# Dense sub-blocks: transposing the raw residual and scaling gate and up by a broadcast row

## The chip, the cores and the metric

One core of one Trainium2 chip runs the whole program. The metric is the device time of one execution in microseconds (us). Engines: TensorE (PE; its weight loads are PEld), VectorE (DVE), ScalarE (ACT), GpSimd (POOL) and SyncE (SP), which issues the weight loads by DMA.

## The reference

The input is 256 tokens of 1024 numbers in float32. Two blocks of two layers follow each other. In the first block each layer is a dense SwiGLU (d_ff 2816), a mixer, and a second SwiGLU, each with an RMS norm before and after it:

```python
def rms_norm(x, g):
    xf = x.astype(jnp.float32)
    return xf * lax.rsqrt(jnp.mean(xf * xf, axis=-1, keepdims=True) + NORM_EPS) * g.astype(jnp.float32)
...
        hdn = swiglu(rms_norm(x, norm_pre[l, 2]), ffn2_w_gate[l], ffn2_w_up[l], ffn2_w_down[l])
        x = x + 0.5 * rms_norm(hdn, norm_post[l, 2])
```

SwiGLU is (silu(h Wg) * (h Wu)) Wd. The norm divides every token by one number, so with r = 1/rms of a token, h Wg = r * ((x*g) Wg), and the same for Wu. The second block (modulated mixers, a dense SwiGLU of 3584, a mixture of eight experts) needs modulation vectors, c_act @ mod_w + mod_b, which are worked out beside the first block.

## The kernel before

The program is a list of ten sub-blocks, `SUBS`: 0, 2, 3 and 5 are the dense SwiGLUs of the first block ("ffn", 22 units of 128 hidden columns each), 1 ("ab") and 4 ("c") its mixers, 6 to 9 the second block. Every engine's instruction stream is written out by hand in program order, with semaphores between them; nothing is rescheduled, so an instruction that waits holds all that stands behind it on its engine.

Every number goes to TensorE as a high and a low part (`XH`, `XL` for the transposed residual, `wh_*`, `wl_*` for weights, `HH`, `HL` for the hidden activations), and each product is three matmuls (`mm3`, L1721 to L1723): high by high, high by low, low by high. A weight block arrives by DMA in `raw_gu` or `raw_d` (two buffers each); ScalarE makes the high part (`hi_gu` L395, `hi_d` L402) and VectorE the low part (`lo_gu` L857, `lo_d` L862).

The start of a dense sub-block b, `pre(b)`:

1. ScalarE squares each of the two token tiles of the residual `X` (`squares`, L413) and takes the root (`root`, L420), then loads the SiLU table (`load_table`, L430).
2. VectorE takes the reciprocal (L948) and writes it on a diagonal, `RS_DIAG` (L954).
3. TensorE multiplies X by that diagonal (L1779): a transpose with the scale in it, 8 pieces of 128 by 128 for each token tile, each of them two passes in the trace. They go to PSUM (`turned`): tile 0 to two banks, tile 1 to four.
4. ScalarE copies each piece to `XH` times the norm's gain (L453), VectorE makes `XL` (L963). They do this in the groups of `TURNS`: four and four pieces of tile 0, then four times two of tile 1. The first gate/up product may begin once the first group of tile 1 is done (`xt_l`).

The loop `ffn`: for unit n TensorE forms gate and up into bank n % 2 of `PB` (`gate_up`, 48 matmuls of 256 columns), ScalarE takes SiLU of the gate (L523), VectorE multiplies it by up (L1070), splits the result (L1071, L1072), and TensorE adds the unit's down product into `PA` (`down`, 12 matmuls of 512 columns). TensorE's order is gate_up(n+1), down(n), so a unit's down product comes a whole gate_up later; only the last down product has no gate_up ahead of it.

GpSimd works out the modulation sums (`modulation`) beside sub-blocks 0, 2, 3 and 4 to 5; it begins them when the transposed residual of that sub-block is complete, in sub-block 0 also after ScalarE's `c_act` (L457). TensorE turns them into columns (`mod_columns`, L1808), behind the last down product of sub-blocks 0, 2 and 3 and ahead of it in sub-block 5. `post(b)` multiplies by the gain, takes the second norm and adds to the residual (L1021, L1025).

Plain transposes, of data that need no diagonal, are at L1781; sub-blocks 6 to 9 use them.

## Time and profile before

| what | value |
|---|---|
| runs (3) | 2750.99, 2751.63, 2753.77 us; median 2751.63 |
| profiled execution, span from first to last instruction | 2747.2 us |
| TensorE busy | 2600.3 us, 95% |
| VectorE, ScalarE, GpSimd busy | 79%, 54%, 34% |
| granted TensorE clock, mean | 0.971 of full |
| loop of sub-block 0, 32 to 206 us | TensorE busy 173.97 of 174.00 us |

The time around the span cannot be read from the trace; the median of the runs stands 4.4 us above the span. TensorE is at work nearly all the time and idle mainly between sub-blocks. A busy share says nothing of whether its clock was full: the column PEclk gives that, as a share of 2.4 GHz.

### The profile page before, as it was taken

What the parts mean: (1) busy time and instruction counts of PE and PEld (TensorE: products, weight loads), DVE (VectorE), ACT (ScalarE), POOL (GpSimd) and SP (SyncE); (2) the same over time, 40 slices, a digit from 0 to 9 for tenths busy, and PEclk for the clock granted to TensorE, in tenths of its full rate; (3) what the DMA queues carried; (4) which work ended last, traced back from release to release, by engine and by line L of the source; (5) the groups of instructions that cost most, each with busy time, mean ns of one, the idle gap of its engine ahead of it and who ended that gap; (6) DMA issues with size and microseconds to landing.
All of it is one profiled execution on the core that took longest, in us unless ns stands there. A gap on an engine that the chain in (4) does not pass through costs nothing. (4 is left out here: it accounts for less than half of the span.)

```text
span 2747.2 us, 47482 instructions
## 1 busy us (share of the span) xinstructions
PE 2600.3 (95%) x17802; PEld 2379.0 (87%) x17802; DVE 2165.5 (79%) x2488; ACT 1483.6 (54%) x1930; POOL 947.8 (34%) x586
## 2 busy tenths in 40 slices
PE   8999899999998998888998978999999999999997
PEld 7999699999897998658998747999999999999986
DVE  5667666766787676987855997898989898989888
ACT  4337543443434334424334515777777777777765
POOL 6990089688789992126900130000000000000000
PEclk9999999999999998999999988999999999999999
DMA  8664267566566653324553415999999999999985
GB/s 309 252 237 148 103 241 256 202 250 254 191 241 229 220 183 134 115 105 164 183 184 138 164 63 192 343 350 333 352 335 349 338 347 343 347 345 346 340 320 216
DMA packets 129209, 670.58 MB, mean 244 GB/s; under 512 B 14672, under 2 KB 14992, under 8 KB 80064
## 3 DMA queue, kind: packets, MB, share of 16 engines
q1 hardware_dynamic: 111024, 604.72, 59.9%
q0 software_dynamic: 18064, 64.21, 6.9%
q8 instruction: 81, 1.33, 0.2%
q14 instruction: 40, 0.33, 0.0%
HBM read 667.82 MB, written 1.05 MB: 243 GB/s over the span
## 5 line engine op out<-in xcount | busy, mean ns | idle before, releaser
L1721 PE MATMUL work<-xT_hi,wh_gu 128*128 128x256 f32 x2088 | 593.9, 284 | 21.6 <-DVE xT_lo L985 12.0
L1722 PE MATMUL work<-xT_lo,wh_gu 128*128 128x256 f32 x2088 | 592.3, 284 | 0.0
L1723 PE MATMUL work<-xT_hi,wl_gu 128*128 128x256 f32 x2088 | 591.7, 283 | 0.0
L1721 PE MATMUL work<-wh_gu,mixT_hi 128*128 128x256 f32 x1792 | 507.5, 283 | 2.8 <-DVE wl_gu L1439 1.5
L1722 PE MATMUL work<-wl_gu,mixT_hi 128*128 128x256 f32 x1792 | 505.8, 282 | 0.0
L1723 PE MATMUL work<-wh_gu,mixT_lo 128*128 128x256 f32 x1792 | 505.5, 282 | 0.0
L857 DVE TENSOR_TENSOR wl_gu<-raw_gu,wh_gu 128x2048 fp32r<-128x2048 f32 x158 | 392.3, 2483 | 72.0 <-ACT wh_gu L395 71.5
L1721 PEld LDWEIGHTS work<-xT_hi,wh_gu 128*128 128x128 f32 x2088 | 401.3, 192 | 30.1 <-issue 21.3
L1722 PEld LDWEIGHTS work<-xT_lo,wh_gu 128*128 128x128 f32 x2088 | 401.7, 192 | 4.8
L1723 PEld LDWEIGHTS work<-xT_hi,wl_gu 128*128 128x128 f32 x2088 | 401.5, 192 | 0.0
L862 DVE TENSOR_TENSOR wl_d<-raw_d,wh_d 128x1024 fp32r<-128x1024 f32 x157 | 250.2, 1594 | 189.6 <-ACT wh_d L402 189.5
L1721 PE MATMUL acc<-wh_d,h_hi 128*128 128x512 f32 x912 | 380.4, 417 | 2.8 <-DVE wl_d L1444 2.7
L1723 PE MATMUL acc<-wh_d,h_lo 128*128 128x512 f32 x912 | 361.2, 396 | 0.0
L1722 PE MATMUL acc<-wl_d,h_hi 128*128 128x512 f32 x912 | 361.1, 396 | 0.0
L1721 PEld LDWEIGHTS work<-wh_gu,mixT_hi 128*128 128x128 f32 x1792 | 340.9, 190 | 12.5 <-DVE wl_gu L1439 1.7
L1722 PEld LDWEIGHTS work<-wl_gu,mixT_hi 128*128 128x128 f32 x1792 | 341.6, 191 | 8.8
L1723 PEld LDWEIGHTS work<-wh_gu,mixT_lo 128*128 128x128 f32 x1792 | 341.5, 191 | 0.0
L402 ACT ACTIVATE wh_d<-raw_d 128x1024 fp32r<-128x1024 f32 x157 | 166.2, 1059 | 276.1 <-PE acc L1723 276.1
L395 ACT ACTIVATE wh_gu<-raw_gu 128x2048 fp32r<-128x2048 f32 x158 | 300.7, 1903 | 25.4 <-PE acc L1723 25.0
L1652 POOL TENSOR_SCALAR scratch<-scratch,small 128x1024 f32<-128x1024 f32 x84 | 312.9, 3724 | 4.2
L1439 DVE TENSOR_TENSOR wl_gu<-raw_gu,wh_gu 128x2048 fp32r<-128x2048 f32 x113 | 259.1, 2293 | 38.0 <-ACT wh_gu L726 37.9
L1439 DVE TENSOR_TENSOR wl_gu<-scratch,wh_gu 128x2048 fp32r<-128x2048 f32 x112 | 256.6, 2291 | 25.5 <-ACT wh_gu L726 25.0
(436 smaller groups left out, 4785.6 us busy)
## 6 DMA issues: line engine op xcount, KB each, us to landing
raw_gu<-in_w_gu SPq DMA_DIRECT2D x271, 1024.0 KB, 5.2
raw_d<-in_w_d SPq DMA_DIRECT2D x269, 512.0 KB, 5.4
scratch<-in_w_gu SPq DMA_DIRECT2D x112, 1024.0 KB, 7.2
scratch<-in_w_d SPq DMA_DIRECT2D x112, 512.0 KB, 7.8
scratch<-in_w_mod POOLq DMA_DIRECT2D x96, 512.0 KB, 3.7
scratch<-in_s_b POOLq DMA_DIRECT2D x16, 256.0 KB, 2.9
rows<-in_norm_post POOLq DMA_DIRECT2D x6, 512.0 KB, 4.4
rows<-in_ln_g POOLq DMA_DIRECT2D x4, 512.0 KB, 5.5
```

The source lines that it names most:

```text
L395: act.activation(wh_gu[k][:, :, :, :].rearrange("p a k n -> p (a k n)"), raw_gu[k][:, :], ACT.Copy).then_inc(gu_hi, 1)
L402: act.activation(wh_d[k][:, :], raw_d[k][:, :], ACT.Copy).then_inc(d_hi, 1)
L857: TT(wl, raw_gu[k][:, :], wh.bitcast(F32), ALU.subtract).then_inc(gu_lo, 1)
L862: TT(wl_d[k][:, :], raw_d[k][:, :], wh_d[k][:, :].bitcast(F32), ALU.subtract).then_inc(d_lo, 1)
L1439: TT(wl, RAW_GU[k] if k > 1 else RAW_GU[k][:, :], wh.bitcast(F32), ALU.subtract).then_inc(gu_lo, 1)
L1652: link(pool.tensor_scalar(MW[n % 3], MW[n % 3], c, None, ALU.mult))
L1721: pe.matmul(out_, w[0], m[0], start=start, stop=False)
L1722: pe.matmul(out_, w[0], m[1], start=False, stop=False)
L1723: return pe.matmul(out_, w[1], m[0], start=False, stop=stop)
```

## The change

In the dense sub-blocks of the first block (`RAW_FFN` = 0, 2, 3, 5):

- TensorE transposes the raw X (plain transposes) as soon as x_in or x_first and x_done allow. There is no `RS_DIAG` for them.
- ScalarE squares tile 0, makes `XH`, then splits the weight block of the sub-block's second unit, squares tile 1, takes both roots and loads the SiLU table.
- VectorE, in its first step, takes both reciprocals behind `lo_gu` of the second unit (`token_scales`). TensorE forms from them a 128 by 256 block with every row the scales of the 256 tokens (`scale_row`, two float32 products into bank 3), between gate_up of the first and of the second unit, and VectorE copies it to `RS_ROW`.
- In every unit VectorE multiplies gate by `RS_ROW` (to `SG`) and up by `RS_ROW` (to `HF`), ScalarE takes SiLU of `SG` in place, and VectorE multiplies the two.
- `mod_columns(1)` moves ahead of the last down product of sub-block 2.

The diff, cut:

```diff
 ScalarE, pre(b)
+                    own_squares(0)
+                    if b not in RAW_FFN:
+                        root(eps_rms, 0)
+                        own_squares(1)
+                        root(eps_rms, 1)
                     if b == 0:
                         act.wait_ge(cols_in, 16)
                         hi_gu(0)
...
+                    if b in RAW_FFN:
+                        hi_gu(START[b] + 1)
+                        own_squares(1)
+                        for t in range(NT):
+                            root(eps_rms, t)
+                        load_table(ACT.Silu)
                     if b == 0:
                         act.activation(c_act, C("c", 0, KD), ACT.Silu).then_inc(c_act_done, 1)
                         hi_d(0)
 ScalarE, ffn
+                        if b in RAW_FFN:
+                            ge(act, gate_scaled, SCALED[b] + n - n0 + 1, at)
+                            act.activation(SG[n % 2], SG[n % 2], ACT.Silu).then_inc(silu_done, 1)
 VectorE
+            def token_scales():
+
+                for t in range(NT):
+                    roots[0] += 1
+                    dve.wait_ge(root_done, roots[0])
+                    dve.reciprocal(rs[:, t:t + 1], rs[:, t:t + 1]).then_inc(rs_ready, 1)
+                scale_rows[0] += 1
+                dve.wait_ge(rs_ps, scale_rows[0])
+                link(dve.tensor_copy(RS_ROW, PB[:, 3, 0:S]))
...
                     lo_gu(n + 1, j)
+                    if first:
+                        token_scales()
+                    if raw:
+                        ge(dve, gu_used, n + 1, j)
+                        TT(SG[k], PB[:, k, 0:S], RS_ROW, ALU.mult).then_inc(gate_scaled, 1)
+                        link(TT(HF[k], PB[:, k, S:2 * S], RS_ROW, ALU.mult))
+                        dve.wait_ge(silu_done, j + (f0 + r + 1))
+                        link(TT(HF[k], SG[k], HF[k], ALU.mult))
 TensorE
+            def scale_row():
+
+                scale_rows[0] += 1
+                pe.wait_ge(rs_ready, NT * scale_rows[0])
+                for t in range(NT):
+                    last = pe.matmul(PB[:, 3, t * P:(t + 1) * P], rs[:, t:t + 1].broadcast_to([P, P]), ident,
+                                     start=True, stop=True)
+                last.then_inc(rs_ps, 1)
...
                 gate_up(n0, dyn)
+                if n0 < START[SECOND]:
+                    scale_row()
                 gate_up(n0 + 1, dyn)
...
-                if n0 == MOD_START[3]:
-                    mod_columns(3)
+                if n0 in (MOD_START[1], MOD_START[3]):
+                    mod_columns(MOD_START.index(n0))
                 down(n0 + nf - 1, dyn, f0 + nf - 1, fdyn, False, True)
-                if n0 in MOD_START[0:3]:
+                if n0 in (MOD_START[0], MOD_START[2]):
```

Where instructions stand, before and after. ScalarE at the program's start, before: squares and roots come first, and behind the pieces of the transposed residual stand `c_act`, the down block of unit 0 and the weight block of unit 1.

```order
L413 ACT_TABLE_LOAD [waits x_in0]
L413 ACTIVATE scratch,small<-residual 128x1024 [waits small_ready]
L420 ACT_TABLE_LOAD
L420 ACTIVATE small<-small 128x1 [waits sq_done]
L413 ACTIVATE scratch,small<-residual 128x1024 [waits sq_done,x_in1]
...
L453 ACTIVATE xT_hi<-acc,cols 128x128
L457 ACTIVATE small<-cols 128x8
L402 ACTIVATE wh_d<-raw_d 128x1024 [waits d_landed0]
L395 ACTIVATE wh_gu<-raw_gu 128x2048 [waits gu_landed1]
L523 ACTIVATE scratch<-work 128x256 [waits gu_used]
```

The same place after:

```order
L466 ACTIVATE xT_hi<-acc,cols 128x128
L404 ACTIVATE wh_gu<-raw_gu 128x2048 [waits gu_landed1]
L422 ACTIVATE scratch,small<-residual 128x1024 [waits sq_done,x_in1]
L429 ACT_TABLE_LOAD
L429 ACTIVATE small<-small 128x1 [waits sq_done] x2
L439 ACT_TABLE_LOAD
L439 ACTIVATE small<-small 128x1 [waits small_ready]
L476 ACTIVATE small<-cols 128x8
L411 ACTIVATE wh_d<-raw_d 128x1024 [waits d_landed0]
L545 ACTIVATE scratch<-scratch 128x256 [waits gate_scaled]
```

The weight block of unit 1 moved ahead of `c_act` and the down block; tile 1's squares, both roots and the table loads moved behind it. VectorE at the program's start, before:

```order
L948 RECIPROCAL small<-small 128x1 [waits root_done,cols_in]
L954 TENSOR_SCALAR scratch<-const,small 128x128 [waits dve_step]
L948 RECIPROCAL small<-small 128x1 [waits root_done]
L954 TENSOR_SCALAR scratch<-const,small 128x128 [waits dve_step]
L857 TENSOR_TENSOR wl_gu<-raw_gu,wh_gu 128x2048 [waits gu_hi]
```

And after, behind the pieces of the transposed residual (`lo_d(0)` stays in `pre`, ahead of the loop's first `lo_gu`):

```order
L989 SCALAR_TENSOR_TENSOR xT_lo<-acc,cols,xT_hi 128x128
L887 TENSOR_TENSOR wl_d<-raw_d,wh_d 128x1024 [waits d_hi]
L882 TENSOR_TENSOR wl_gu<-raw_gu,wh_gu 128x2048 [waits gu_hi]
L1090 RECIPROCAL small<-small 128x1 [waits root_done] x2
L1093 COPY scratch<-work 128x256 [waits rs_ps]
```

Both reciprocals stand behind the two weight pieces now; before they were VectorE's first work. TensorE from the last down product of sub-block 2 to the first product of sub-block 3, before:

```order
L1722 MATMUL acc<-wl_d,h_hi 128x512
L1723 MATMUL acc<-wh_d,h_lo 128x512
L1808 MATMUL work<-small,scratch 128x1 [waits mod_sums]
L1808 MATMUL work<-small,scratch 128x1 x23
L1779 MATMUL work<-scratch,residual 128x128 [waits xn_done]
L1779 MATMUL work<-scratch,residual 128x128 x7
L1779 MATMUL work<-scratch,residual 128x128 [waits mod_copied,xn_done]
```

After:

```order
L1855 MATMUL work<-small,scratch 128x1 [waits mod_sums]
L1855 MATMUL work<-small,scratch 128x1 x23
L1765 MATMUL acc<-wh_d,h_hi 128x512 [waits h_ready,d_lo]
L1766 MATMUL acc<-wl_d,h_hi 128x512
...
L1767 MATMUL acc<-wh_d,h_lo 128x512
L1828 MATMUL work<-const,residual 128x128 [waits x_first]
L1828 MATMUL work<-const,residual 128x128 x7
L1828 MATMUL work<-const,residual 128x128 [waits mod_copied,x_done]
```

The 24 column products moved from behind the last down product to ahead of it, and the transposes wait for the residual itself.

## Rows read from the trace of the kernel before

**Rows 1.** Page, busy us (share of the span) x instructions of each engine.

```profile
PE 2600.3 (95%) x17802; PEld 2379.0 (87%) x17802; DVE 2165.5 (79%) x2488; ACT 1483.6 (54%) x1930; POOL 947.8 (34%) x586
```

**Rows 2.** Loop of sub-block 0: busy by stretch, then VectorE groups (busy, mean ns).

```profile
32.00:206.00 174.00, 173.97 (x1215) 162.28 (x1214) 115.72 (x101) 67.44 (x63) 159.67 (x64) 1.00 0.69 250
...
L1072 DVE TENSOR_TENSOR h_lo<-scratch,h_hi 128x256 fp32r<-128x256 f32 x20 | 9.4, 471 | 0.7
L1070 DVE TENSOR_TENSOR scratch<-scratch,work 128x256 f32<-128x256 f32 x20 | 8.4, 419 | 13.4 <-ACT scratch L523 13.4
```

**Rows 3.** Timeline of the start: start us, duration us, engine, line, [idle before].

```profile
9.89 1.28 ACT L430 ACT_TABLE_LOAD   x1
...
17.19 1.17 ACT L402 ACTIVATE wh_d<-raw_d 128x1024 fp32r<-128x1024 f32 x1
...
18.72 1.92 ACT L395 ACTIVATE wh_gu<-raw_gu 128x2048 fp32r<-128x2048 f32 x1 [0.36 <-DMA raw_gu<-in_w_gu]
...
19.57 1.22 DVE L862 TENSOR_TENSOR wl_d<-raw_d,wh_d 128x1024 fp32r<-128x1024 f32 x1
...
20.70 2.29 DVE L857 TENSOR_TENSOR wl_gu<-raw_gu,wh_gu 128x2048 fp32r<-128x2048 f32 x1
...
24.28 0.39 ACT L523 ACTIVATE scratch<-work 128x256 f32<-128x256 f32 x1 [3.64 <-PE work L1723]
```

**Rows 4.** Timeline of the seam into sub-block 2, ScalarE and TensorE.

```profile
339.39 1.06 ACT L413 ACTIVATE scratch<-residual 128x1024 f32<-128x1024 f32 x1
...
340.57 0.29 ACT L420 ACTIVATE small<-small 128x1 f32<-128x1 f32 x1
...
343.76 1.13 ACT L453 ACTIVATE xT_hi<-work,cols 128x128 fp32r<-128x128 f32 x4
...
348.30 0.36 PE L1721 MATMUL work<-xT_hi,wh_gu 128*128 128x256 f32 x1
```

**Rows 5.** Stretches: length, busy PE, PEld, DVE, ACT, POOL; PEclk, DMA share, GB/s.

```profile
341.50:346.80 5.30, 5.29 (x25) 5.29 (x25) 1.87 (x8) 4.79 (x15) 0.18 (x1) 0.50 0.29 99
...
1058.50:1063.80 5.30, 5.30 (x13) 3.80 (x13) 1.99 (x6) 0.98 (x2) 0.00 (x0) 0.50 0.00 0
...
1074.20:1078.10 3.90, 3.88 (x18) 3.90 (x19) 2.62 (x6) 3.64 (x5) 0.55 (x1) 0.50 0.22 58
...
1249.10:1252.20 3.10, 3.07 (x14) 3.10 (x15) 1.82 (x6) 2.70 (x4) 0.00 (x0) 0.50 0.00 0
...
1504.30:1508.20 3.90, 3.83 (x18) 3.87 (x19) 2.62 (x6) 3.68 (x5) 0.00 (x0) 0.50 0.00 0
```

**Rows 6.** Timeline of the seam into sub-block 5, VectorE and TensorE.

```profile
856.18 3.18 DVE L1025 SCALAR_TENSOR_TENSOR residual<-scratch,small,residual 128x1024 f32<-128x1024 f32 x1
...
867.53 0.36 PE L1721 MATMUL work<-xT_hi,wh_gu 128*128 128x256 f32 x1 [0.22 <-DVE xT_lo L963]
...
869.88 3.57 DVE L857 TENSOR_TENSOR wl_gu<-raw_gu,wh_gu 128x2048 fp32r<-128x2048 f32 x1 [0.95 <-ACT wh_gu L395]
```

**Rows 7.** Timeline of TensorE at the seams into sub-blocks 3 and 6.

```profile
536.14 0.39 PE L1808 MATMUL work<-small,scratch 128*128 128x1 f32 x3
...
550.56 0.36 PE L1721 MATMUL work<-xT_hi,wh_gu 128*128 128x256 f32 x1 [0.44 <-DVE xT_lo L963]
...
1052.82 0.39 PE L1808 MATMUL work<-small,rows 128*128 128x1 f32 x3
...
1066.83 0.44 PE L1781 MATMUL work<-const,residual 128*128 128x128 f32 x2 [2.84 <-DVE residual L1025]
```

**Rows 8.** Timeline at the end of sub-block 0, VectorE and TensorE.

```profile
202.93 0.43 DVE L1072 TENSOR_TENSOR h_lo<-scratch,h_hi 128x256 fp32r<-128x256 f32 x1
...
203.50 0.47 PE L1721 MATMUL acc<-wh_d,h_hi 128*128 128x512 f32 x1
...
207.16 0.38 PE L1808 MATMUL work<-small,scratch 128*128 128x1 f32 x2 [0.62 <-POOL small L1657]
```

**Rows 9.** Timeline of GpSimd, the end of the sums that sub-block 2 covers.

```profile
528.55 0.10 POOL L1657 MEMSET small<- 128x1 f32 x1
```

94 lines of the change are left out of this document (53 added, 41 removed).

## The prediction

> **What bounds the kernel now.** I read the page's busy shares first: TensorE 95% of the span, the others 79% or less [rows 1]. Then the same by stretch: inside the loop of a dense sub-block TensorE has no idle time at all and VectorE is busy 116 of 174 us, some 5.7 us in a unit of 8.5 us (20 units and a bit in 174 us) [rows 2]. So inside the loops nothing on VectorE counts until it takes more than the spare 2.8 us. What the change can give or take lies where TensorE stands still: the program's start and the seams into sub-blocks 2, 3 and 5. There I read the timeline, engine by engine, in order of time. All sums are made against the profiled execution, span 2747.2 us. The median of the three runs is 2751.63, 4.4 us more, and I add the sum to it. About 0.2% (5.5 us) is the least that a measurement of this kernel tells from no change.
>
> **What moves.** The transposes no longer wait for square, root, reciprocal and diagonal. In exchange three things become new: a wait of TensorE for both reciprocals between the first and the second gate/up product; three vector operations in each unit where there was one; and modulation columns ahead of the last down product of sub-block 2.
>
> **Program start (sub-block 0).** Before, ScalarE's piece of the second weight block starts at 18.72 us, held by its DMA, and VectorE's piece of 2.29 us starts at 20.70; it is done at 22.99, ahead of the end of the first product, which the SiLU at 24.28 shows (0.26 us after its last matmul issued, so the second product began at 24.0) [rows 3]. The raw transposes start earlier, but the first product still needs the first weight block to land and be split; I take 17.9 for its start, and two us more or less would change nothing, since the second product is held by something else: the new order on ScalarE. Behind the second weight block (18.7 to 20.6) now stand the squares of token tile 1 (1.06 plus 0.19), a table load of 1.28, two roots (0.5), a second table load 1.28 with its one-column use 0.2, the small SiLU (0.1 apart) and only then the first down block (1.17): 20.6 + 1.15 + 1.3 + 0.5 + 1.3 + 0.2 + 0.1 + 1.2 = 26.3 us [rows 3, 4]. VectorE is in order too: its piece of that down block (1.22) is placed ahead of its piece of the second weight block (2.29), and both ahead of the reciprocals. So 26.3 + 1.2 + 2.25 + 0.3 = 30.05 us until TensorE may make the scale row, and about 0.45 more until the second product: 30.5 against 24.0, **+6.5 us**. Before, the same vector pieces were covered by the first product; that cover (it ends by 24 to 25.5) is now too short by six. The loads behind them come earlier than they are needed, by more than that.
>
> **The clock.** TensorE's granted clock stood at half (1.2 GHz) through most of each seam. In sub-blocks 1 to 5 the diagonal products, two passes each and 32 in all, ran at half speed and it was back at full (2.4 GHz) when the first product began: 0.50 from 341.5 to 346.8, then the product from 348.30 at full [rows 4, 5]. At the three seams of before that use plain transposes, one pass each, the clock came back only within the first product: 3.9, 3.1 and 3.9 us of it were at 0.50 (18, 14 and 18 matmuls there, not the double) [rows 5]. Half of that is lost, 1.8 us. I take this price for the seams into 2, 3 and 5, and once for the start, where TensorE would stand idle some 5 to 7 us ahead of its second product. The least that it could be is 0, if the shorter pause between transposes and product keeps the clock up; the most is 2.6 (5.3 us at half, rows 5, first row). I choose 1.8, since those three rows are of the same form. Start: +6.5 + 1.8 = **+8.3**.
> The Trainium skill says it as a rule ("TensorE: Matmul & The Clock Gate", Part 4: PE-mode transpose): transposes in that mode do not count as busy work for the clock as matmuls do. The rows of the three seams agree with it; by that rule these 1.8 us are paid at every seam, and without it none.
>
> **Scale row.** Two fp32 products of 128 columns, four passes. At full clock such passes stand 0.11 to 0.12 us apart, at half 0.21: 0.45 to 0.85 us, of which I take 0.45. Nothing hides it, it stands between two products. Zero is no bound, since the passes are TensorE's own.
>
> **Seam into sub-block 2.** The residual of tile 0 is written by 339.39. ScalarE squares it and is free at 340.57 [rows 4]; in the new order its pieces of the transposed residual start then, where they started at 343.76 behind roots and table load. Sixteen at 0.285 follow without a break. VectorE takes each group of four, four and two after ScalarE at 0.28 each, and the product may begin when the tenth is done: 4.05 us behind ScalarE's start. That is 344.7 against 348.30 [rows 4], -3.6. The roots now end at 345.3 + 1.9 + 1.25 + 0.5 = 349.0 and VectorE's piece of the weights at 349.5, reciprocals 349.9, the first product at 350.5 at the earliest: covered. Sum -3.6 + 1.8 + 0.45 = **-1.35**.
>
> **Seam into sub-block 5.** The first half of the residual is ready by 856.1; the second add takes 3.18 us, beside GpSimd, until 859.36 [rows 6]. ScalarE, after 1.2 us of squares, starts at 857.3 with tile 0, tile 1 can be transposed from 859.4, its first group is ready about 860.05, split at 861.3: the product at 861.3 against 867.53, -6.2 [rows 6]. Its second weight block (3.57 us under contention, from 864.4) is done at 868.0, the reciprocals at 868.4, the first product with its half-clock part at 868.9: just covered. Sum -6.2 + 1.8 + 0.45 = **-3.95**.
>
> **Seam into sub-block 3.** Here the modulation columns ran behind the last down product (from 536.14 on), mostly under the residual chain [rows 7]. They now stand ahead of that product. Sub-block 5 has this order already: columns from 1052.82, last down product at half clock from 1058.5 (13 matmuls in 5.3 us, where twelve take 2.8 of a unit in the loops), residual ready and first transpose at 1066.83 [rows 5, 7]. That is 14.0 us. With it, from the end of the previous down product (533.4) the residual is ready at 547.4, ScalarE starts its pieces at 548.65 and the product begins at 552.7, against 550.56 [rows 7]: +2.1. So what the raw transposes give (about 5.7) is spent on bringing 5.7 us of columns and 2.1 us of slow clock into the path. Sum 2.1 + 1.8 + 0.45 = **+4.35**. GpSimd's sums are in at 528.55 [rows 9], before the 532 or so at which they would be wanted.
>
> **Inside the loops.** Each unit gets gate times row and up times row (PSUM and SBUF in, 0.42 as L1070) and gate times up from SBUF (0.42 to about 1.3, as L1072: 20 of them mean 0.47, few are long) for one 0.42: +0.85 to +1.7 us of VectorE in 8.5, where 2.8 were free [rows 2]. The result is needed a whole product later, so inside the loop this costs 0. Only the last unit has no such cover: its last vector step ended at 203.36 and the down product waited for it until 203.50, some 0.2 us late [rows 8]. The chain is longer by scale, 0.45, and the second multiplication, 0.45: **+0.9** at the end of sub-block 0, and the same in sub-block 3 (same phase). Bounds 0 and 2 us each. Sub-blocks 2 and 5 have the columns as cover.
>
> **Sum.** +8.3 - 1.35 + 4.35 - 3.95 + 1.8 = **+9.15 us**: span 2756.4, median 2751.63 + 9.15 = 2760.8.
>
> **Rivals.** (1) *The clock comes back in time*: four times 1.8 fall away, +1.95, 2753.6 us, no difference. For it: the pause between transposes and product shrinks to some 2 us from 4. Against it: three seams out of three. This is the not-slower side; it decides whether the sum passes 5.5. (2) *GpSimd becomes the bound*: the modulation sums are ready just as TensorE wants them (it waited 0.62 us for them at 207.16 [rows 8]). The new multiplication of two SBUF tensors falls beside GpSimd's work 22 times, up to 0.42 us each, so up to 9 us for each of three modulations. In sub-blocks 0 and 3 TensorE comes later than before by some 4.1 and 3.1 us, counted from GpSimd's start; less the old wait of 0.6 that leaves 3.5 and 2.5 of slack, in 2 some 7. Fully paid it is 5.5 + 6.5 + 2 = 14 more, 2775; half paid, with the slack used first, 1 + 2 = 3 more, 2764. Against it: VectorE's long pieces, 2.3 and 1.2 us, do most of the blocking already.
> The Trainium skill ("SBUF — State Buffer", Who interferes with whom) says that a vector operation with two SBUF inputs contends with a GpSimd one that reads SBUF, and one with a single SBUF input does not. By that one new operation in three counts, and the rows agree: L1070, with PSUM, kept its 419 ns on the mean of 20 while L1072, with two from SBUF, rose to 471 ns.
> (3) *A gain*: the start is not held (ScalarE or the DMA faster than I think) and rival 1 holds too: -4 to -6 us, 2747.
>
> **Chances.** Forecast 0.55, clock back in time 0.23, GpSimd bound 0.17, gain 0.05. The range runs from rival 1's low side to half of GpSimd's price with slower seams: 2752 to 2773. Faster by over 0.2% 0.04, within 0.2% 0.26, slower 0.70.
>
> **What would show it.** The first product of sub-block 0 ends near 24 to 25.5 and the second starts near 30.5, with VectorE's down-block piece ahead of the weight piece. Granted clock 0.5 in the first 3 to 4 us of the products at the seams into 2, 3 and 5. Columns ahead of sub-block 2's last down product, which takes near 5 us. A gap of about 1 us before the last down product of 0 and 3. No new idle time in the loops. I am wrong if the second product of sub-block 0 starts by 26, if the clock is full at the seams, or if TensorE waits long for the modulation sums.

## The result, and the profile after

The changed kernel is slower. Side by side, five runs each, it took 2763.01, 2774.99, 2769.17, 2765.81 and 2764.71 us (median 2765.81) against a median of 2750.99 us (2750.43 to 2753.77) for the kernel before: ratio 1.0051, 95% interval 1.0031 to 1.0072. In experiment 12, eight more runs of the same kernel had a median of 2759.83 against 2748.00, ratio 1.0039 (1.0021 to 1.0056), with runs from 2756.04 to 2774.04. (The ratios are those on record with the runs; they are not always the quotient of the two medians.) The forecast was 2760.8 in a range of 2752 to 2773, slower with 0.70. So the forecast sign came true, and the size is 11.8 to 14.8 us where 9.15 was forecast.

The profiled execution of the changed kernel took 2763.01 us, span 2761.2, mean granted clock 0.966 (before 2747.2 and 0.971). Its page, the line that answers to [rows 1]:

```profile
PE 2605.7 (94%) x17754; PEld 2381.8 (86%) x17754; DVE 2246.4 (81%) x2660; ACT 1484.4 (54%) x1930; POOL 968.1 (35%) x586
```

TensorE has 5.4 us more of busy time with 48 fewer instructions: a part of the loss is slower clock, the rest idle time. VectorE has 172 instructions and 81 us more, and GpSimd, whose program did not change, has 20 us more.

**Where the 14.0 us of span are.** I cut both traces at TensorE's own instructions: from the last down product of a sub-block to the first transpose (T) of the next, from T to the first gate/up product, the first two products, and the rest. "First two products" in sub-blocks 2, 3 and 5 includes the scale row of the new kernel.

| stage | before | after | difference | forecast |
|---|---|---|---|---|
| start to the second product's end, sub-block 0 | 29.7 | 37.2 | +7.5 | +8.3 |
| rest of 0 to the end of its down products | 176.4 | 176.9 | +0.5 | +0.9 |
| seam into 1 (GpSimd wait, columns) | 8.24 | 7.98 | -0.25 | 0 |
| sub-block 1 | 115.05 | 116.55 | +1.5 | 0 |
| seam into 2, to the first product | 12.11 | 8.30 | -3.8 | -3.6 |
| first two products of 2 | 11.47 | 13.38 | +1.9 | +2.25 |
| rest of 2, columns and last down product in it, and seam into 3 to T | 184.02 | 192.98 | +9.0 | |
| T to the first product of 3 | 6.76 | 5.14 | -1.6 | |
| these two rows together | | | +7.3 | +2.1 |
| first two products of 3 | 11.47 | 13.70 | +2.2 | +2.25 |
| rest of 3 | 176.40 | 176.87 | +0.5 | +0.9 |
| seam into 4, and sub-block 4 | | | -0.8 | 0 |
| seam into 5, to the first product | 15.57 | 10.27 | -5.3 | -6.2 |
| first two products of 5 | 11.71 | 13.88 | +2.2 | +2.25 |
| all that is left | | | +0.6 | 0 |

The rows differ from the forecast by less than 1 us except in two places: sub-block 1, and everything between the first product of 2 and the first of 3. There the sum was +2.1 and the trace has +7.3. (The row of sub-block 1 is counted from its first product. A second profile of the same kernel, experiment 12, has +5.5 in the second place and none of the 1.5 in sub-block 1.)

**The start.** Timeline of the changed kernel (start us, duration us, engine, line, [idle before]), against [rows 3]:

```profile
18.55 1.91 ACT L404 ACTIVATE wh_gu<-raw_gu 128x2048 fp32r<-128x2048 f32 x1 [1.29 <-DMA raw_gu<-in_w_gu]
20.36 1.04 ACT L422 ACTIVATE scratch<-residual 128x1024 f32<-128x1024 f32 x1
21.52 1.28 ACT L429 ACT_TABLE_LOAD   x1
22.81 0.48 ACT L429 ACTIVATE small<-small 128x1 f32<-128x1 f32 x2
23.31 1.28 ACT L439 ACT_TABLE_LOAD   x1
24.81 1.04 ACT L411 ACTIVATE wh_d<-raw_d 128x1024 fp32r<-128x1024 f32 x1
25.89 1.22 DVE L887 TENSOR_TENSOR wl_d<-raw_d,wh_d 128x1024 fp32r<-128x1024 f32 x1 [6.21 <-ACT wh_d L411]
27.03 2.28 DVE L882 TENSOR_TENSOR wl_gu<-raw_gu,wh_gu 128x2048 fp32r<-128x2048 f32 x1
29.23 0.21 DVE L1090 RECIPROCAL small<-small 128x1 f32<-128x1 f32 x2
29.50 0.79 PE L1863 MATMUL work<-const,small 128*128 128x128 f32 x4 [3.10 <-DVE small L1090]
29.96 0.54 PE L1765 MATMUL work<-xT_hi,wh_gu 128*128 128x256 f32 x1
```

This is the forecast chain, link by link: squares, two table loads and roots on ScalarE, then its piece of the down block at 24.81, then VectorE's two pieces. VectorE stood idle for 6.21 us ahead of `lo_d`, although the weight block behind it in its queue had been there since 20.5. TensorE waited 3.10 us for the reciprocals. The second product began at 29.96; the forecast said 30.5.

**The clock.** Stretches at the beginning of the products (length, then busy us and count of PE, PEld, DVE, ACT, POOL; granted clock, DMA share, GB/s): after the scale row in sub-block 0, and at the first product of 2, of 3 and of 5.

```profile
29.90:33.40 3.50, 3.50 (x19) 3.50 (x19) 2.75 (x7) 2.16 (x3) 2.90 (x3) 0.51 0.94 384
353.70:357.70 4.00, 4.00 (x21) 4.00 (x22) 3.40 (x7) 3.95 (x7) 1.58 (x3) 0.57 0.25 65
565.20:569.40 4.20, 4.18 (x20) 4.20 (x21) 3.95 (x11) 4.15 (x7) 1.57 (x3) 0.51 0.29 83
878.80:883.20 4.40, 4.38 (x20) 4.40 (x21) 3.88 (x7) 4.35 (x7) 3.71 (x4) 0.50 0.01 4
```

All four stand at or near half (0.50 to 0.57, 1.2 GHz is 0.50), with about 20 matmuls in 4 us where the full clock does 33 (experiment 3 shows that). This is what [rows 5] showed of the seams with plain transposes before.

**The columns of sub-block 2.** TensorE between the last two down products of 2, a window over the columns, and the seam into 3:

```profile
543.85 0.38 PE L1855 MATMUL work<-small,scratch 128*128 128x1 f32 x2 [0.58 <-POOL small L1701]
...
552.72 0.78 PE L1765 MATMUL acc<-wh_d,h_hi 128*128 128x512 f32 x1
...
565.22 0.55 PE L1765 MATMUL work<-xT_hi,wh_gu 128*128 128x256 f32 x1 [1.47 <-DVE xT_lo L989]
```

```profile
543.80:552.60 8.80, 8.75 (x48) 8.75 (x48) 1.98 (x4) 2.11 (x3) 0.00 (x0) 0.59 0.40 155
```

TensorE waited for GpSimd's sums (0.58 us before the first column product), then the 24 column products (48 passes) took 8.9 us, most of them at half clock, where the forecast put 5.7 from sub-block 5's order. The wait alone does not decide that: in the second profile of the same kernel the same 0.58 us stand ahead of them and they take 6.7 us, and the whole place costs 5.5 instead of 7.3.

**Inside the loop.** The stretch of [rows 2] in the new kernel, and VectorE's groups in it (busy us, mean ns | idle before):

```profile
32.00:206.00 174.00, 174.00 (x1224) 163.29 (x1224) 132.17 (x145) 68.06 (x62) 159.25 (x64) 1.00 0.70 251
...
L1113 DVE TENSOR_TENSOR scratch<-scratch 128x256 f32<-128x256 f32 x21 | 17.2, 820 | 4.7 <-ACT scratch L545 4.7
L1118 DVE TENSOR_TENSOR h_lo<-scratch,h_hi 128x256 fp32r<-128x256 f32 x21 | 13.3, 632 | 0.7
L1110 DVE TENSOR_TENSOR scratch<-work,scratch 128x256 f32<-128x256 f32 x20 | 8.5, 424 | 6.8 <-PE work L1767 6.2
```

TensorE still has no idle time there, as forecast. VectorE rose from 115.7 to 132.2 us. The multiplication of PSUM by SBUF (L1110) costs 424 ns; that of two SBUF tensors (L1113) 820 ns, about twice as much, and `h_lo` went from 471 to 632 ns. So VectorE's operations with two SBUF inputs are longer here; experiment 5 shows that this is GpSimd's doing. The next question is what GpSimd pays in return.

### The profile page after: what moved, and what is told of

Its sections match the earlier page's. It is cut to its first block and busy times, and to the rows that moved or that the text cites. A ratio compares the mean times of both kernels' runs of the same rounds, so it can differ in the third digit from the quotient of the medians.

```text
span 2761.2 us, 47645 instructions
## 1 busy us (share of the span) xinstructions
PE 2605.7 (94%) x17754; PEld 2381.8 (86%) x17754; DVE 2246.4 (81%) x2660; ACT 1484.4 (54%) x1930; POOL 968.1 (35%) x586
## 5 line engine op out<-in xcount | busy, mean ns | idle before, releaser
L1696 POOL TENSOR_SCALAR scratch<-scratch,small 128x1024 f32<-128x1024 f32 x84 | 321.4, 3826 | 4.2
```

What stands on the lines that cost most here:

```text
L1696: link(pool.tensor_scalar(MW[n % 3], MW[n % 3], c, None, ALU.mult))
```

## What was to be told apart

My theory after the first result: the sum of the forecast is right term by term, the start and the columns are the cost, the seams give back about what the clock takes. The rivals: (a) the clock term is not caused by the plain transposes, (b) the start would not matter, since something else (GpSimd's sums) is late anyway, (c) GpSimd's sums get slower through VectorE's extra work in the loops, and this costs more than any single seam. Twelve experiments were made, one of them the changed kernel again, on three chips: 1 to 4 on one, 5, 6, 8 and 9 on another, 10 to 13 on a third. Each is compared with the kernel before on its own chip, and a difference taken across chips is rough. Each is shown with the stages it was made for; "first T of 6" is the time of sub-block 6's first transpose, the end of all that the change touches.

### Experiment 1: the down block ahead

```diff
 ScalarE, pre(b), raw
+                        if b == 0:
+                            hi_d(0)
                         hi_gu(START[b] + 1)
                         own_squares(1)
...
                     if b == 0:
                         act.activation(c_act, C("c", 0, KD), ACT.Silu).then_inc(c_act_done, 1)
-                        hi_d(0)
```

> The changed kernel, with one move on ScalarE in sub-block 0: the high part of unit 0's down block is made ahead of the weight block of unit 1, not behind squares, roots and table loads. My theory (the order on ScalarE and VectorE at the start costs 6 us and a stretch at half clock): the second product starts near 24.5 instead of 29.96 us, the scale row near 24.2, and the time falls by 5 to 7 us against the changed kernel. Rival (the start is held by the roots themselves, at 23.6 us plus two reciprocals): it falls by 5 at most. Rival (the loss is elsewhere and the start is made good later): no difference.

Measured: median 2777.16 us (6 runs, 2759.5 to 2780.5) against 2747.42, ratio 1.0085 (1.0060 to 1.0110). The expectation was 5 to 7 us less than the changed kernel; it is slower than that, 29.7 us above the kernel before. The profiled execution (span 2778.6): the second product, and then TensorE at the seams into 1 and 4, where it takes GpSimd's sums, with a window over the columns at the first:

```profile
26.02 0.36 PE L1766 MATMUL work<-xT_hi,wh_gu 128*128 128x256 f32 x1
...
214.25 0.37 PE L1856 MATMUL work<-small,scratch 128*128 128x1 f32 x1 [5.98 <-POOL small L1702]
...
761.80 0.37 PE L1856 MATMUL work<-small,scratch 128*128 128x1 f32 x1 [5.90 <-POOL small L1702]
```

```profile
214.20:224.50 10.30, 10.24 (x48) 10.25 (x49) 3.57 (x7) 2.81 (x6) 3.48 (x4) 0.50 0.33 53
```

The start did what it should: the second product at 26.02 instead of 29.96, at a better clock, 31.7 us to its end instead of 37.2. All of it and more was lost 180 us later. TensorE came to the seam earlier and stood still for 5.98 us for GpSimd's sums, and after that pause the columns ran at 0.50 for 10.3 us. The seam took 16.6 us against 8.0. At the seam into 4 the same happened (16.6 against 7.8), and a further 6.5 us of this profile stand behind the first T of 6 (1687.4 against 1680.9), of which experiment 12 says more. So rival (b) was true for this kernel, in a form that I had not priced: the wait costs its length and then again the clock of the columns behind it.

### Experiment 2: the columns of sub-block 2 behind again

```diff
-                if n0 in (MOD_START[1], MOD_START[3]):
+                if n0 == MOD_START[3]:
                     mod_columns(MOD_START.index(n0))
                 down(n0 + nf - 1, dyn, f0 + nf - 1, fdyn, False, True)
-                if n0 in (MOD_START[0], MOD_START[2]):
+                if n0 in MOD_START[0:3]:
```

> The changed kernel with mod_columns(1) put back behind the last down product of sub-block 2. My theory (columns ahead lengthen the path): the seam into sub-block 3, from the end of the last but one down product to the first product 22.4 us long in the changed kernel, shrinks to 16 to 18 us, and the time falls by 4 to 6.5 us; the wait of 1 us for the sums goes too. Rival (they are as long on the path behind as ahead, since the transposes now wait for nothing else): within 1 us.

Measured: median 2754.64 us (12 runs, 2751.93 to 2770.32), ratio 1.0022 (1.0010 to 1.0033). The stage that is undone, in the profile: rest of sub-block 2 from 189.6 to 177.9 us; the residual chain to T from 3.37 to 7.17, since the columns now run in it. From the second product of 2 to the first of 3 that is 198.1 us in the changed kernel and 190.2 here, a gain of 7.9 us, close to the 7.3 us that the ledger gives to this place (against the changed kernel's second profile, 196.3, the gain is 6.1). TensorE at the columns of 2, and at the seam into 4:

```profile
545.37 0.28 PE L1855 MATMUL work<-small,scratch 128*128 128x1 f32 x2
...
751.77 0.37 PE L1855 MATMUL work<-small,scratch 128*128 128x1 f32 x1 [5.91 <-POOL small L1701]
```

There is no wait for the sums any more at 545.37. The profiled execution is the slowest of the twelve, and shows why: it waits 5.91 us at the seam into 4, while the eleven others have no profile. The median stands 7.2 us above the kernel before, where the changed kernel stands 11.8 to 14.8 above: this edit takes back some 5 to 8 us, about half of the loss. So the place of the columns costs as much as the start. The forecast had +2.1 for this stage against the kernel before, and with the columns behind the stage takes 190.2 us where that kernel took 190.8: nearly all of the +7.3 is the columns' place.

### Experiment 3: raw transposes as two-pass products

```diff
-                            last = pe.transpose(turned(t, k), src[:, t, cols_k], ident)
+                            if b in RAW_FFN:
+                                last = pe.matmul(turned(t, k), src[:, t, cols_k], ident, start=True, stop=True)
+                            else:
+                                last = pe.transpose(turned(t, k), src[:, t, cols_k], ident)
```

> The changed kernel with its transposes of the raw residual made as float32 products with the identity, two passes each as the diagonal products before, not as plain transposes. Theory A (plain transposes do not keep the clock up, products do): the granted clock is 1.0 in the first product of sub-blocks 2, 3 and 5, each saving 1.5 us there; the transposes end later, by 3 us, so the time moves little (-2 to +3 us). Theory B (it is the pause before the first product that lets the clock fall, whatever the transposes are): the clock in the first products stays at half for 3 to 4 us and the time grows by 2 to 5 us.

Measured: median 2769.71 us (6 runs, 2762.56 to 2772.49), ratio 1.0071 (1.0056 to 1.0087). That is 22.3 us above the kernel before, some 7 to 10 more than the changed kernel, where -2 to +3 was expected; why is not shown, since the profiled execution is the fastest of the six. But the stage for which it was made answers clearly. Stretches at the first product of 2, 3 and 5:

```profile
352.20:356.20 4.00, 4.00 (x33) 4.00 (x34) 3.32 (x7) 3.95 (x7) 1.59 (x3) 1.00 0.27 100
565.60:569.60 4.00, 4.00 (x33) 4.00 (x34) 3.75 (x11) 3.95 (x7) 1.57 (x3) 1.00 0.27 101
878.00:882.00 4.00, 3.99 (x33) 4.00 (x34) 3.04 (x7) 3.95 (x9) 3.31 (x4) 1.00 0.00 0
```

Full clock at all three, 33 matmuls in 4.00 us against 20 to 21, and the first two products take 11.90 us at each seam instead of 13.38, 13.70 and 13.88: 1.5, 1.8 and 2.0 us, the price of 1.8 that the forecast took. Against that stand 0 to 1.3 us for the second passes (T to product 6.02, 6.43 and 6.10, against 5.08, 5.14 and 6.11). In the profile part of the saving goes in sub-block 2: its rest was 191.8 us here (189.6 in the changed kernel), and TensorE waited 3.64 us for the sums ahead of its columns:

```profile
541.47 0.29 PE L1858 MATMUL work<-small,scratch 128*128 128x1 f32 x1 [3.64 <-POOL small L1701]
```

The Trainium skill has this as a rule ("TensorE: Matmul & The Clock Gate", Part 4: PE-mode transpose): transposes in that mode don't count as TensorE being busy in the way that matmuls do. The three pairs of stretches agree with it. But the price is not paid every time in these runs: at the seam into 3 the two products took 11.9 us with plain transposes too in the profiles of experiments 1, 2, 8 and 13 and in the changed kernel's second profile, against 13.7 in its first and 13.1 in experiment 5. What decides it there stays open.

### Experiment 4: raw transposes in sub-blocks 2 and 5 only

```diff
-        RAW_FFN = [b for b in range(SECOND) if SUBS[b][0] == "ffn"]
+        RAW_FFN = [2, 5]
...
-                if n0 in (MOD_START[1], MOD_START[3]):
+                if n0 == MOD_START[3]:
```

Sub-blocks 0 and 3, and the place of the columns, are as before.

> Only sub-blocks 2 and 5 transpose the raw residual and scale gate and up by the row; 0 and 3 are as in the kernel before, and mod_columns(1) stands behind the down product. By the stages read from the two traces: seam 2 -3.8, first products +1.9, first down product's wait +2.4, seam 5 -5.3, first products +2.2: -2.6 us against the kernel before, 2748 to 2750. Rival (the saving at each seam is eaten by half clock and GpSimd, different in each run): 2751 to 2756 with a wider spread.

Measured: median 2752.11 us (12 runs, 2743.25 to 2754.3) against 2747.42, ratio 1.0006 (0.9995 to 1.0018): no gain. The median is 4.7 us higher, as the rival had it (2751 to 2756); five runs lie at 2743 to 2749 and seven at 2752 to 2754, and the profile is of the fastest. Both seams gave what the changed kernel gave there (TensorE's first product of 5 in this kernel):

```profile
357.50 0.47 PE L1768 MATMUL acc<-wh_d,h_hi 128*128 128x512 f32 x1 [1.66 <-DVE h_lo L1121]
...
859.11 0.55 PE L1768 MATMUL work<-xT_hi,wh_gu 128*128 128x256 f32 x1 [0.83 <-DVE xT_lo L992]
```

Seam into 2: 8.31 us to the first product against 12.11, two products 13.16 against 11.47, and then 178.5 us for the rest of 2 against 176.1, with the first line above in it: TensorE waited 1.66 us ahead of the first down product. So of 3.8 us that the raw transposes save in 2 they lose 1.7 to the clock and 2.4 in the units behind: nothing is left. Seam into 5: 10.26 against 15.57, two products 14.09 against 11.71, a gain of 2.9. First T of 6 is at 1059.64 against 1066.83, but of that 1.4 us in sub-block 1 and 1.65 at the seam into 4 are in stretches that this kernel shares with the one before.

### Experiments 5, 6 and 8: GpSimd cut short

The modulation's two operations work on 64 instead of 1024 columns in all three, so the modulation is left out but for its loads and a small part; DMA traffic, semaphores and TensorE's columns stay.

```diff
-                        link(pool.tensor_scalar(MW[n % 3], MW[n % 3], c, None, ALU.mult))
-                        TT(acc, acc, MW[n % 3], ALU.add).then_inc(mod_term, 1)
+                        link(pool.tensor_scalar(MW[n % 3][:, 0:64], MW[n % 3][:, 0:64], c, None, ALU.mult))
+                        TT(acc[:, 0:64], acc[:, 0:64], MW[n % 3][:, 0:64], ALU.add).then_inc(mod_term, 1)
```

On the changed kernel:

> The changed kernel with the same cut of GpSimd's modulation work (modulation vectors incomplete). Theory (part of the changed kernel's loss, and its spread over runs, is GpSimd being slowed by and slowing VectorE's new work): against the kernel before with the same cut it is slower by 8 to 10 us only, not 14 to 20, runs agree within 2 to 3 us, the first down product of sub-block 2 waits no longer, and VectorE's units in the loop show no operation above 0.45 us of 256 columns. Rival (the loss is the order at the seams alone): the difference stays 14 us or more.

On the kernel before:

> The kernel before, with GpSimd's modulation work cut: of each 1024-column multiplication and addition behind the first of a sum only 64 columns are computed, so the modulation vectors are incomplete; all waits and loads stay. It is the base for the next two. GpSimd then ends each modulation long before TensorE wants it and hardly meets VectorE: the waits of 0.6 us for the sums go, and the residual add at the seam into sub-block 5 takes 1.3 us instead of 3.2, the diagonals 0.3 instead of 1.2: 3 to 5 us faster than the kernel before.

On experiment 1's kernel:

> The changed kernel with the down block of unit 0 made first on ScalarE at the start, and GpSimd's modulation work cut as in the two others (modulation vectors incomplete). Theory (moving that block saves 5.5 us of TensorE at the start, and with the full work GpSimd gives it back as a wait for its sums at the end of sub-block 0): here it is 5 to 7.5 us faster than the changed kernel with the same cut. Rival (the start is made good elsewhere): within 2 us.

Measured on one chip, where the kernel before took 2753.63 us:

| kernel, GpSimd short | runs | median (range) us | ratio to before |
|---|---|---|---|
| before | 10 | 2750.35 (2741.21 to 2754.74) | 0.9974 (0.9961 to 0.9986) |
| changed | 10 | 2754.51 (2750.09 to 2761.40) | 1.0001 (0.9988 to 1.0014) |
| down block ahead | 9 | 2749.72 (2746.07 to 2753.90) | 0.9984 (0.9972 to 0.9997) |

Three things follow. First, without GpSimd's work the change costs 4.2 us of median, 7.4 by the two ratios, and 8.9 between the fastest runs (2750.09 and 2741.21). With it, in the two comparisons above, they are 11.8 to 14.8, 10.7 to 14.0, and 10.6 (experiment 12, 2756.04 and 2745.39). So some part of the loss goes through GpSimd, from 2 to 11 us by the measure that one takes; these runs do not say how much. What GpSimd adds is above all the upper part of the runs, those that reach 2760 to 2778; with GpSimd short no run passed 2761.4. They spread over 11 us all the same, where 2 to 3 was expected.

Second, the start is a real cost. With GpSimd short the down block ahead saves 4.8 us of median (5 to 7.5 expected), and its profile reaches the first T of 6 at 1061.52 instead of 1069.86. That the same edit made a loss in experiment 1 therefore comes with GpSimd's full work.

Third, VectorE's groups in sub-block 2 (stretch 361 to 530), in the changed kernel with GpSimd short:

```profile
L1113 DVE TENSOR_TENSOR scratch<-scratch 128x256 f32<-128x256 f32 x21 | 10.7, 508 | 4.3 <-ACT scratch L545 4.3
L1118 DVE TENSOR_TENSOR h_lo<-scratch,h_hi 128x256 fp32r<-128x256 f32 x20 | 8.6, 431 | 0.7
```

and, from the changed kernel with full GpSimd, its `h_lo` (stretch 367 to 540):

```profile
L1118 DVE TENSOR_TENSOR h_lo<-scratch,h_hi 128x256 fp32r<-128x256 f32 x21 | 17.6, 836 | 0.7
```

Beside a GpSimd that hardly works `h_lo` takes 431 ns, beside a working one 836. That is contention, and it doubles the operation. The first unit of sub-block 2, full GpSimd, VectorE's two-input operations and then TensorE's first down product:

```profile
363.09 1.67 DVE L1113 TENSOR_TENSOR scratch<-scratch 128x256 f32<-128x256 f32 x1 [0.22 <-ACT scratch L545]
...
366.39 2.55 DVE L1118 TENSOR_TENSOR h_lo<-scratch,h_hi 128x256 fp32r<-128x256 f32 x1
...
369.08 0.47 PE L1765 MATMUL acc<-wh_d,h_hi 128*128 128x512 f32 x1 [1.72 <-DVE h_lo L1118]
```

5.85 us from the start of the first to the end of the last of three operations, of which with GpSimd short the first and the last average 0.51 and 0.43 us. There the same product starts without a wait:

```profile
365.94 0.40 PE L1765 MATMUL acc<-wh_d,h_hi 128*128 128x512 f32 x1
```

### Experiments 10 and 11: the kernel before with nothing but more work on VectorE

In every unit of the first block's dense sub-blocks, on the kernel before, behind the wait for SiLU; the results are thrown away. Experiment 10 adds three multiplications as the change's (two of PSUM by SBUF, one of two SBUF tensors), experiment 11 only the first two.

```diff
                     dve.wait_ge(silu_done, ...)
+                    TT(view(1024, 256), PB[:, k, 0:S], view(512, 256), ALU.mult)
+                    TT(view(1280, 256), PB[:, k, S:2 * S], view(512, 256), ALU.mult)
+                    TT(view(1536, 256), view(512, 256), view(768, 256), ALU.mult)
```

> The kernel before, with three operations more on VectorE in each unit of sub-blocks 0, 2, 3 and 5, between SiLU and its product: two that read PSUM and one SBUF tile, and one with two SBUF inputs; their results are not used, the output is the same. Theory (the loop's new operations cost TensorE nothing inside the loop, but prolong GpSimd's modulations, which TensorE waits for at the ends of sub-blocks 0 and 3): TensorE's loops keep 176.1 us, GpSimd's modulations of 179 to 187 us grow to 187 to 193, and the seams into 1 and 4 grow by 3 to 9 us each, 3 to 15 us in all. Rival (GpSimd is prolonged by the moved seams alone): within 2 us of the kernel before.

> As the one above, but only the two operations that read PSUM and one SBUF tile, without the one with two SBUF inputs. Theory (only an operation with two SBUF inputs meets GpSimd): GpSimd's modulations keep their 179 to 187 us, and the time is within 2 us of the kernel before. Rival (what counts is where VectorE's long weight pieces fall against GpSimd's steps, and any shift moves that): they change as in the one above.

Measured against 2748.00 us: experiment 10 a median of 2774.81 (4 runs, 2771.43 to 2777.81), ratio 1.0093 (1.0073 to 1.0113); experiment 11 2768.60 (4 runs, 2768.0 to 2778.07), ratio 1.0081 (1.0059 to 1.0103). This is as much as the whole change or more (3 to 15 us were expected), from operations for which VectorE has the time and whose results nobody uses. The loop of sub-block 0 in experiment 11 (as [rows 2]), then TensorE at its seam into 4 and a window over the columns there:

```profile
32.00:206.00 174.00, 173.78 (x1214) 162.16 (x1213) 126.23 (x147) 66.27 (x62) 159.76 (x63) 1.00 0.68 247
...
754.50 0.37 PE L1816 MATMUL work<-small,scratch 128*128 128x1 f32 x1 [6.10 <-POOL small L1665]
```

```profile
754.50:764.60 10.10, 10.10 (x48) 10.10 (x48) 3.13 (x7) 2.80 (x6) 0.61 (x1) 0.50 0.15 52
```

In the loops TensorE loses nothing. The loss is at the seams into 3 and 4, not into 1 and 4 as expected: 16.8 us each in both kernels (last down product to T), against 7.9 and 8.3 before. That is 17.5 of the 24.4 us by which the profile of experiment 10 is longer, and 17.4 of 18.7 in experiment 11. Each is a wait of 6.1 to 6.2 us for the sums and columns at half clock. The sums' length, from GpSimd's first load to its last step:

| kernel | beside 0 | beside 2 | beside 3 | beside 4 and 5 |
|---|---|---|---|---|
| before | 186.9 | 178.6 | 187.2 | 182.0 |
| changed, first profile | 189.4 | 188.4 | 189.4 | 186.8 |
| changed, second profile (12) | 189.4 | 188.1 | 192.6 | 180.7 |
| 1, down block ahead | 189.5 | 190.1 | 192.6 | 180.6 |
| 10, before and three more | 189.6 | 192.7 | 192.8 | 182.8 |
| 11, before and two more | 188.4 | 192.3 | 192.3 | 182.2 |
| 3, two-pass transposes | 189.4 | 187.5 | 187.6 | 186.4 |
| 13, down block and `c_act` ahead | 188.6 | 188.2 | 187.6 | 186.4 |
| 4, raw in 2 and 5 | 180.9 | 190.0 | 178.6 | 187.4 |
| 9, raw in 5 | 179.9 | 187.1 | 187.1 | 186.2 |

Before, the sums beside 2 took 178.6 us to 528.55 [rows 9], and TensorE wanted them at 536.14 [rows 7], 186.2 us after GpSimd's start: no wait. With 192 us GpSimd is the bound. But 178.6 is not what the old code always takes. In the first three columns, the sums beside sub-blocks that are as before took 178.6 to 187.2 us (the rows "before" and 9, and row 4 beside 0 and 3), and beside changed ones 187.5 to 192.8. So the added operations cost between nothing and some 14 us for one set of sums. Where the time goes can be seen in its groups, beside sub-block 3, before (stretch 551 to 740) and in experiment 10 (562 to 761):

```profile
L1652 POOL TENSOR_SCALAR scratch<-scratch,small 128x1024 f32<-128x1024 f32 x21 | 84.7, 4033 | 1.1
L1653 POOL TENSOR_TENSOR scratch<-scratch 128x1024 f32<-128x1024 f32 x21 | 59.6, 2836 | 1.8
```

```profile
L1662 POOL TENSOR_SCALAR scratch<-scratch,small 128x1024 f32<-128x1024 f32 x21 | 88.2, 4199 | 1.1
L1663 POOL TENSOR_TENSOR scratch<-scratch 128x1024 f32<-128x1024 f32 x21 | 63.0, 3000 | 1.7
```

The two steps of a round, 4.03 and 2.84 us, become 4.20 and 3.00: 0.33 us more in each of the 21 rounds shown, 7 us. The first step of a round has in the main one of two lengths, 2.85 us or 4.8, the longer where most of VectorE's `lo_gu` (2.28 us) lies inside it. Two neighbouring rounds of the kernel before, where `lo_gu` starts at 576.75 and 585.24, and two of experiment 11, where it starts at 595.81 and 604.30:

```profile
576.95 4.78 POOL L1652 TENSOR_SCALAR scratch<-scratch,small 128x1024 f32<-128x1024 f32 x1
...
585.43 4.80 POOL L1652 TENSOR_SCALAR scratch<-scratch,small 128x1024 f32<-128x1024 f32 x1
```

```profile
596.01 4.79 POOL L1660 TENSOR_SCALAR scratch<-scratch,small 128x1024 f32<-128x1024 f32 x1
...
604.51 4.79 POOL L1660 TENSOR_SCALAR scratch<-scratch,small 128x1024 f32<-128x1024 f32 x1
```

Experiment 11 was to decide which of the new operations does it, and it refutes the price that I had put on them in the prediction. The Trainium skill ("SBUF — State Buffer", Who interferes with whom) has contention only where VectorE uses the port pair that it shares with GpSimd, so two operations with one SBUF input each should leave GpSimd alone. For the single step that holds: in the rounds above `lo_gu` and the short operations behind it lie inside the step in both kernels, those with a PSUM input take 0.42 us of it before and 1.25 us in experiment 11, and the step is as long, 4.8 us. Such an operation is not lengthened beside GpSimd either (L1110, 424 ns). But GpSimd's sums were as long with these two alone, 192.3 us, as with all three, 192.7.

The reading that fits both is that it counts how VectorE's `lo_gu` falls into GpSimd's rounds, and that any operation beside it moves that. The two rhythms lock: the rounds shown start 8.48 and 8.50 us apart, the starts of `lo_gu` 8.49, and it is so for most rounds of a dense sub-block, where with GpSimd short most rounds take 2 to 5 us. They fall out of step here and there, and also at the end. The first steps of the last two rounds beside sub-block 3 start 5.66 us apart in the kernel before and in the changed kernel's first profile, and 8.5 us apart in experiments 10 and 11 and in the changed kernel's second profile. That one interval is 2.8 to 2.9 us of the difference between 187.2 or 189.4 and 192.3 to 192.8 us. What decides whether it is the short or the long one is not shown, since no run moved VectorE's pieces by a chosen time.

### Experiment 12: the changed kernel again

It is the changed kernel without an edit, on the chip and beside the runs of experiments 10, 11 and 13.

> The changed kernel itself once more, on the chip of the others of this call. 12 to 18 us slower than the kernel before; its runs spread over 10 us or more, and the two that differ most in time differ in the waits for GpSimd's sums.

Measured: median 2759.83 us, and eight runs in two groups: four at 2756.0 to 2757.2, four at 2762.4 to 2774.0. Its profile is the slowest of them (span 2772.2, 11.0 more than the first profile of the same program):

```profile
755.49 0.37 PE L1855 MATMUL work<-small,scratch 128*128 128x1 f32 x1 [5.91 <-POOL small L1701]
```

The seam into 4 takes 16.6 us in this profile and 7.8 in the first one: 8.8 us by this one wait and its slow columns. So the same program sometimes pays at a seam and sometimes not. Two things together make the wait 5.9 us instead of 0.2: GpSimd's sums beside sub-block 3 took 192.6 instead of 189.4 us, and TensorE, at full clock behind the transposes this time, came to them 2.5 us sooner after GpSimd's start (186.7 instead of 189.3). The 11.0 us are a balance: up to the last down product of 3 the second profile is 6.6 us ahead of the first, the seam costs it 8.8, the stretch from there to the first T of 6 another 2.4, and what follows 6.4. That last part is code that is the same in all kernels; from the first T of 6 to the end the profiles show either 1680.4 to 1682.8 or 1687.1 to 1687.4 us. The longer time stands in four of the eight profiles with raw transposes in all four sub-blocks and in none of the six others, so I cannot say that the change has no part in it. No profile fell into the lower group of runs, 2756 to 2757.

### Experiment 13: down block ahead, and GpSimd's start ahead too

```diff
 ScalarE, pre(b), raw
+                        if b == 0:
+                            act.activation(c_act, C("c", 0, KD), ACT.Silu).then_inc(c_act_done, 1)
+                            hi_d(0)
                         hi_gu(START[b] + 1)
```

In experiment 1 and in the changed kernel GpSimd begins at 24.7 and 25.2 us, held by `c_act`, which stands behind squares, roots and table loads; before, it began at 20.2.

> The changed kernel with the down block of unit 0 first at the start, as before, and with the SiLU of c_act (GpSimd's first input) ahead of it, at the price of one table load more. Theory (the gain at the start was given back because GpSimd began its sums no earlier, at 24.7 us): GpSimd begins near 20 us, its sums of sub-block 0 are in near 209.5, and TensorE's wait for them falls from 6.3 to under 2 us; the seam into sub-block 1 falls from 16.6 to 8 to 12 us. The time is 4 to 9 us below that of the kernel with the down block first alone. Rival (GpSimd's steps are locked to the units of the loop, so an earlier start wins nothing): no difference.

Measured: median 2753.61 us (12 runs, 2749.89 to 2777.72), ratio 1.0035 (1.0014 to 1.0056). GpSimd's first load, TensorE's second product and its first column product:

```profile
19.64 1.57 POOL L1686 DMA_DIRECT2D scratch<-in_w_mod  x3 [15.59 <-DVE xT_lo L989]
...
25.16 0.36 PE L1765 MATMUL work<-xT_hi,wh_gu 128*128 128x256 f32 x1
...
208.33 0.38 PE L1855 MATMUL work<-small,scratch 128*128 128x1 f32 x2
```

The wait of 5.98 us is gone (seam into 1: 7.73 us instead of 16.64), with the start's gain kept (30.9 us to the end of the second product, against 37.2), and the last down product of 3 comes at 743.66, against 755.79 and 749.18 in the two profiles of the changed kernel. The second is the fair comparison, 5.5 us, because it had the same columns in sub-block 2 and the same clock at the seam into 3; the first T of 6, at 1067.42 instead of 1080.31 or 1084.92, has in it that this profile paid no wait at the seam into 4. Experiment 1 paid there too, so its distance of 23.6 us of median to this kernel, where 4 to 9 was expected, is not all `c_act`. The seam into 1 is the missing half of experiment 1. On this chip the median is 6.2 us below the changed kernel's (experiment 12), though the two ratios' intervals overlap: seven of the twelve runs lie at 2749.9 to 2755.2, where the changed kernel has none, but four at 2767 to 2778, with one at 2759 between. That these four pay at a seam is my guess from their distance; no trace shows it.

### Experiment 9: raw transposes in sub-block 5 only, as two-pass products

As experiment 4, with `RAW_FFN = [5]` and the product of experiment 3. It takes the one seam that paid, leaves out what GpSimd's sums of 0, 2 and 3 see, and keeps the clock.

> Only sub-block 5 transposes the raw residual and scales by the row, and its transposes are two-pass products with the identity; all else as in the kernel before. From the stages: seam 5 and its first two products took 27.3 us before and 22.2 in the kernel with two-pass transposes: 5 us faster than the kernel before, with its spread. If the products of the row do not keep the gain (first down product waits for VectorE under contention): 2 to 3 us faster. Rival (the gain is lost in the loop of sub-block 5 by VectorE's two more operations): no difference.

Measured: median 2749.31 us (12 runs, 2746.09 to 2758.78) against 2753.63, ratio 0.9988 (0.9975 to 1.0001). TensorE's first product of 5 and the stretch behind it:

```profile
864.89 0.35 PE L1768 MATMUL work<-xT_hi,wh_gu 128*128 128x256 f32 x1 [1.21 <-DVE xT_lo L992]
...
864.90:868.90 4.00, 4.00 (x33) 4.00 (x34) 3.33 (x7) 3.95 (x7) 3.40 (x3) 1.00 0.02 3
```

The residual is ready for TensorE after 4.16 instead of 8.78 us, T to product 6.59 against 6.79, two products at full clock 11.90 against 11.71 with the scale row in them: 4.6 us saved. That is 0.17% of the program. The expectation was 5 us, the median is 4.3 us lower, but the interval includes 1, and I do not call it faster. It is the only version with the whole computation whose median is below the kernel before's.

## Why the prediction came out as it did

**The start: right, in mechanism and size.** The step "26.3 + 1.2 + 2.25 + 0.3" gave 30.5 for the second product, the trace 29.96, by the same chain. The clock beside it (0.51 for the first 3.5 us) came as priced. Experiments 8 and 13 undid it: 4.8 us of median with GpSimd short, and 6.3 us at the end of the second product. What the step did not see is that the same order also holds GpSimd's start (`c_act`), 5 us later than before.

**Seams into 2 and 5, and the clock: right to the end of the first two products.** -3.8 and -5.3 to the first product against -3.6 and -6.2, +1.9 and +2.2 behind it against 2.25. In sub-block 2 the first down product then waits 1.7 us for `h_lo`, which the sum did not have. Rival 1, the clock back in time, fell at all three seams of the changed kernel's first profile, and experiment 3 shows that the kind of transpose makes the difference in these profiles.

**Seam into 3: right sign, mis-sized.** The term "+2.1" measured +7.3. It took the columns' 5.7 us from sub-block 5's order, where they do not wait and start at full clock. In sub-block 2 they came after a wait of 0.6 us for the sums and took 8.9 us in the first profile, and the wait ahead of the first down product of the sub-block (1.7) is in the same stage. In the second profile the columns took 6.7 us behind the same wait, and the term is +5.5. So some 2 us of the miss are the state of the clock in one profile. The sentence that GpSimd's sums, in at 528.55 [rows 9], are early for a use at 532 was the weak one: 3.5 us of slack (rival 2 counts some 7 there), and the prediction's own rival 2 was enough to use it up.

**"Inside the loops this costs 0": wrong, through GpSimd.** For TensorE and VectorE it holds (TensorE busy 174.00 of 174.00 us). But the operations that cost their own engine nothing lengthen GpSimd's sums, to 187.5 to 192.8 us where the old code took 178.6 to 187.2. Experiments 10 and 11 put such operations alone on the kernel before and lost 26.8 and 20.6 us of median.

**Rival 2: true in part of the runs, and too low in its price for one seam.** It was given 0.17 and priced at 2764 half paid, 2775 fully paid. The changed kernel's runs lie at 2756 to 2775, so it is not one outcome but a mixture. The price per seam was set at the wait alone; the runs show the wait of about 6 us and, in a seam 8.6 to 8.9 us longer, some 2.7 us of slower columns behind it. The reason given against it (VectorE's long pieces do most of the blocking already) is true of the single step and did not exclude a loss, since what changes, as far as the traces show it, is how many rounds are in step with those pieces. The reason given for its size, that only the new operation with two SBUF inputs counts, was wrong: the sums are as long without it.

**Sub-block 1 (+1.5): not forecast, not tested.** A stretch at half clock lasted 10.2 us instead of 6.8 in it. Sub-block 1 takes 113.5 to 116.5 us in all kernels, the one before among them with 115.05, so I put no cause on it. The changed kernel's second profile has 115.1.

In sum the forecast was near in part by luck: its missing term, GpSimd's wait at a seam, is absent from the first profile, and where it is paid the runs reach 2774 against the 2760.8 of the forecast. It was made of the right parts at the start and at the seams, and of a wrong zero in the loops.

## What to carry to other kernels

Work on an engine with time to spare is free only if no engine beside it gets slower by it; ask of every engine that runs alongside how much slack it has at the next place where it is waited for. A wait of TensorE costs its length and what the clock takes from the work right behind it, so sums 3.2 us longer on a side engine, met 2.5 us sooner, cost 8.8 us (experiment 12). When a stream is reordered, follow each small instruction in it to what it releases: one activation of 128 by 8 numbers, moved by 5 us, decided between a stall of 6 us at the next seam and none (experiments 1 and 13).
